# Shared expert's row tiles inside the expert loop, a shorter route, group conditions; narrow blocks' weights fetched by transfers that the scalar engine issues

## What is computed

```
def swiglu(x, w_gate, w_up, w_down):
    return (jax.nn.silu(x @ w_gate) * (x @ w_up)) @ w_down
...
def moe_ffn(h, router_w, router_bias, w_gate, w_up, w_down, ws_gate, ws_up, ws_down):
...
    affinity = jax.nn.sigmoid((h @ router_w).astype(f32))
    _, idx = lax.top_k(affinity + router_bias.astype(f32), TOP_K)
    s_sel = jnp.take_along_axis(affinity, idx, axis=-1)
    gates = s_sel / jnp.sum(s_sel, axis=-1, keepdims=True) * ROUTED_SCALE
...
    def expert_block(acc, blk):
        tok, g, e = blk
        y = swiglu(h_ext[tok], w_gate[e], w_up[e], w_down[e])
        return acc.at[tok].add(y * g[:, None]), None
...
    return acc[:n_tok] + swiglu(h, ws_gate, ws_up, ws_down)
...
        x = x + g2 * moe_ffn(h2.reshape(-1, dm), *moe_w).reshape(x.shape)
```

## Time and profile before

| what | us |
|---|---|
| runs | 2946.36, 2951.84, 2951.17 |
| median | 2951.17 |
| profiled execution, its own time | 2948.95 |
| its span | 2947.2 |
| PE busy | 2262.6 (77%) |
| DVE, ACT, POOL busy | 965.4, 602.9, 569.8 |
| HBM traffic | 628 MB read, 95 MB written |

### The profile page before, as it was taken

One profiled execution on the slowest core, in us unless ns is written; L12 is line 12 of the kernel. 1 busy time (PEld: TensorE's weight loads), 2 busy tenths in 40 slices (PEclk: granted clock), 3 DMA queues, 4 the chain that ended last, 5 costly groups with the idle time before them and its releaser, 6 DMA issues. The chain is left out here.

```text
span 2947.2 us, 41851 instructions
## 1 busy us (share of the span) xinstructions
PE 2262.6 (77%) x12118; PEld 1306.1 (44%) x12119; DVE 965.4 (33%) x2075; ACT 602.9 (20%) x1018; POOL 569.8 (19%) x470
## 2 busy tenths in 40 slices
PE   3995997669596999999999406339966999988881
PEld 2893543444343444444444206337433444444441
DVE  4742237662322111211111146861232111111113
ACT  2232224330211121212212004021021211211110
POOL 2540000000102222222222130400001222222322
PEclk9998999879797999999999757557987999999996
DMA  9983100100509999999999274314035999999994
GB/s 321 353 292 129 57 29 0 72 1 0 211 36 357 347 363 349 367 353 355 357 354 327 77 241 156 80 48 170 0 154 229 378 357 353 364 335 392 391 382 145
DMA packets 177204, 684.02 MB, mean 232 GB/s; under 512 B 34298, under 2 KB 36794, under 8 KB 132346
## 3 DMA queue, kind: packets, MB, share of 16 engines
q1 hardware_dynamic: 129642, 581.86, 51.3%
q0 software_dynamic: 38848, 71.14, 10.1%
q10 hardware_dynamic: 8624, 29.82, 2.5%
HBM read 628.15 MB, written 94.65 MB: 245 GB/s over the span
## 5 line engine op out<-in xcount | busy, mean ns | idle before, releaser
L1369 PE MATMUL pGUw_m<-wguw_m,xTw_m 128*128 128x512 f32 x800 | 358.6, 601 | 21.8 <-issue 21.8
L1380 PE MATMUL pGUn_m<-wgun_m,xTn_m 128*64 128x256 f32 x2816 | 323.3, 382 | 27.9 <-issue 27.9
L1380 PEld LDWEIGHTS pGUn_m<-wgun_m,xTn_m 128*64 128x64 f32 x2816 | 210.9, 137 | 171.7 <-issue 98.2
L1369 PEld LDWEIGHTS pGUw_m<-wguw_m,xTw_m 128*128 128x128 f32 x800 | 149.1, 191 | 232.7 <-issue 232.7
L1419 PE MATMUL pYn_m<-wdn_m,hidTn_m 128*64 128x512 f32 x704 | 189.9, 615 | 19.0 <-DVE hidTn_m L1324 16.6
L1398 PE MATMUL pYw_m<-wdw_m,hidTw_m 128*128 128x512 f32 x400 | 191.8, 602 | 15.5 <-DVE hidTw_m L1310 15.5
L1173 POOL DMA_INDIRECT xgw_m<-moe_h,idxw_m x58 | 60.4, 1042 | 652.1 <-PE pTw_m L1355 619.7
L819 POOL MEMSET zero_r<- 128x1024 f32 x2 | 1.9, 951 | 793.2 <-POOLq L69 523.7
L1179 POOL DMA_INDIRECT xgn_m<-moe_h,idxn_m x96 | 101.1, 1054 | 249.9 <-DVE idxn_m L1300 212.0
L1200 POOL DMA_INDIRECT moe_acc<-yn_m,idxn_m x88 | 140.5, 1597 | 27.5 <-issue 27.5
L1307 DVE TENSOR_TENSOR hidw_m<-hsilw_m,pGUw_m 128x256 f32<-128x256 f32 x50 | 21.1, 421 | 329.2 <-ACT hsilw_m L1242 329.2
(11 more groups left out here) (378 smaller groups left out, 3498.8 us busy)
## 6 DMA issues: line engine op xcount, KB each, us to landing
wgun_m<-in_exp_w_gate SPq DMA_DIRECT2D x88, 1024.0 KB
wgun_m<-in_exp_w_up SPq DMA_DIRECT2D x88, 1024.0 KB
wdn_m<-in_exp_w_down SPq DMA_DIRECT2D x88, 1024.0 KB
wguw_m<-in_exp_w_gate SPq DMA_DIRECT2D x50, 1024.0 KB
wguw_m<-in_exp_w_up SPq DMA_DIRECT2D x50, 1024.0 KB
wdw_m<-in_exp_w_down SPq DMA_DIRECT2D x50, 1024.0 KB
w_p<-in_mod_w SPq DMA_DIRECT2D x24, 2048.0 KB
acc_c<-moe_acc SPq DMA_DIRECT2D x30, 512.0 KB, 10.8
```

The costliest lines, as they stand in the source:

```text
L1369: last = pe.matmul(pGU_w[:], xT_w[b % 2][:, k, :], wgu[0][b % WIDE_RING][:, :, k, :], start=(k == 0), stop=(k == KD - 1))
L1380: last = pe.matmul(pGU_n[H * side:H * side + H, b % 2], xT_n[b % 2][:, k % 4, H * (k // 4):H * (k // 4) + H], w[:, :, k, P * side:P * side ...
```

## The change

- **Route.** The shared expert leaves it. PE waits for the router's two loads only (`wload` at 32), and logits of tile t-1 follow the transposes of tile t. `moe_acc` is zeroed in `mixer0`, by six transfers of SP (15.7 MB) that follow the load of the output weights; each layer has accumulators of its own. The table no longer passes DRAM: eight matmuls by the identity move it to one partition of PSUM, and DVE copies it. The copies that split the gates stand behind the table.
- **Loop.** A whole trip stands under `If(n_both > 6q)`, n_both being the larger item count. The shared expert writes `moe_shared`: its tile 0 in the prologue (row transposes first, `up` one k at a time between the picks, `down` behind them), its tile q+1 in trip q at block 3, with PE behind `rest_narrow`; ACT and DVE have it last in the block. For it the step `wide_stored`, which holds a wait at block 3 alone, stands under an `If` in every block.
- **Narrow weights.** Their ring has 2 buffers instead of 3, and ACT issues them: gate and up behind `silu_narrow`, down behind Y's evacuation, each under an `If` with a table load. The first two narrow items' six transfers are the first thing ACT does in the block.
- **Buffers.** Wide rows have 2 buffers instead of 3, `y_w` one instead of two, narrow `pGU` one; the narrow picks share a bank with it.
- **Combine.** It has four parts; PE adds three of them by the identity in PSUM (12 instructions a tile) in place of POOL; loads of tile t>=2 wait for tile t-2's sum.
- **Prepare.** The four groups' `pK` matmuls write to four column groups of the array, with the group as the innermost loop; ACT copies them in four pieces, and the stored table is 120 KB instead of 60 KB a half batch.

```diff
-WIDE_RING, NARROW_RING = 2, 3
+WIDE_RING, NARROW_RING = 2, 2
+SHARED_AT = 3
...
-            sp.wait_ge(tab_done, 1)
-            sp.dma_start(tab_dram, tabi[:]).then_inc(tab_out, 16)
-            sp.wait_ge(tab_out, 16)
-            sp.dma_start(table[:], tab_dram[0:ROWS, :].rearrange("(o a) b -> o (a b)", o=1)).then_inc(tab_in, 16)
-            for t in range(NT):
-                sp.wait_ge(y_done, t + 1)
-                sp.dma_start(accs[0][t * P:(t + 1) * P, :], ysh[:, t % 2, :]).then_inc(y_out[t % 2], 16)
...
-            act.wait_ge(zero_done, 1)
-            for acc in accs[1:]:
-                for t in range(NT):
-                    act.dma_start(acc[t * P:(t + 1) * P, :], zero[:]).then_inc(zero_out, 16)
...
+            rows(0)
+            pe.wait_ge(wload, 32)
+            for t in range(1, NT):
+                rows(t)
+                logits(t - 1)
+            logits(NT - 1)
...
+            for c in range(8):
+                last = pe.matmul(pTab[:, c, 0:ROWS], tabf[:, c:c + 1], ident[:, 0:ROWS], start=True, stop=True)
+            last.then_inc(tab_mm, 1)
...
+            n_both = eng.value_load(table[0:1, 3:4], min_val=(NT - 1) * UNROLL, max_val=max(most_wide, NE))
...
+                with eng.If(n_both > q * UNROLL):
...
+                            elif b == kind - 2:
+                                with eng.If(q < NT - 1):
+                                    step(q)
...
+                with act.If(n_narrow > i + NARROW_RING):
+                    gate_up_narrow(expert(act, 1, i + NARROW_RING), b % NARROW_RING)
...
+                act.wait_ge(yw_added, i * 16 + 32)
+                act.activation(y_w[:], pY_w[:], ACT.Copy, scale=gslot[0][b][:]).then_inc(W['y_done'], 1)
...
+                with act.If(n_narrow > i + NARROW_RING):
+                    down_narrow(expert(act, 1, i + NARROW_RING), b % NARROW_RING)
...
+            def shared_rows(t):
+                for half in range(2):
+                    act.wait_ge(Z['xT_mm'], t * 2 + 1 + half)
+                    act.activation(xT_s[:, 4 * half:4 * half + 4, :], pT_w[:].rearrange("p (k c) -> p k c", c=P),
+                                   ACT.Copy).then_inc(Z['xT_done'], 1)
...
+                act.wait_ge(Z['gu_mm'], t + 1)
+                act.activation(hsil_w[:], pGU_w[:, 0, :], ACT.Silu).then_inc(Z['silu_done'], 1)
+                act.wait_ge(Z['y_mm'], t + 1)
+                act.activation(xy_s[:], pY_w[:], ACT.Copy).then_inc(Z['y_done'], 1)
...
+            for b in range(NARROW_RING):
+                with act.If(n_narrow > b):
+                    gate_up_narrow(expert(act, 1, b), b)
+                    down_narrow(expert(act, 1, b), b)
...
+            shared_rows(0)
+            shared_rest(0)
...
+            def shared_head(q):
+                shared_rows(q + 1)
+                for k in range(KD):
+                    last = shared_up(k)
+                last.then_inc(Z['gu_mm'], 1)
...
+            def wide_stored(i, q, b):
+                if b == SHARED_AT:
+                    pe.wait_ge(W['y_done'], i + 2)
...
+            shared_rows(0)
             for i in range(AHEAD):
                 for kind in range(2):
+                    if i:
+                        pe.wait_ge(S[kind]['idx_done'], i)
                     pick(kind, i)
-                    pe.wait_ge(S[kind]['idx_done'], i + 1)
+                    last = shared_up(2 * i + kind)
+            last.then_inc(Z['gu_mm'], 1)
+            for kind in range(2):
...
+            trips(pe, n_wide, n_narrow,
+                  ((0, up_wide), (1, up_narrow), shared_at(SHARED_AT + 1, shared_stored), (0, rest_wide), (1, rest_narrow),
+                   shared_at(SHARED_AT, shared_head), (0, wide_stored), shared_at(SHARED_AT, shared_tail)))
...
+                if t >= 2:
+                    sp.wait_ge(summed, t - 1)
+                for k in range(4):
+                    sp.dma_start(slot(k, t), parts[k][t * P:(t + 1) * P, :]).then_inc(acc_in[t], 16)
...
+                pe.wait_ge(acc_in[t], 64)
+                if t >= 2:
+                    pe.wait_ge(summed, t - 1)
+                for half in range(2):
+                    c = slice(half * 512, (half + 1) * 512)
+                    for k in range(1, 4):
+                        last = pe.matmul(pS[t % 2][:, c], ident[:], slot(k, t)[:, c], start=(k == 1), stop=(k == 3))
+                last.then_inc(part_sum, 1)
...
+                dve.tensor_tensor(total[t % 2][:], slot(0, t), pS[t % 2][:], ALU.add).then_inc(summed, 1)
...
-                    for g in range(4):
-                        gg = n * GB + 4 * half + g
-                        for d, k0, c0 in ((1, 1, 0), (0, 0, 7 * SI)):
-                            for part in range(2):
-                                last = pe.matmul(pK[0:SI, g * 256 + c0:g * 256 + c0 + SL * SI], Bd[d][:, part, gg, :],
+                    for d, k0, c0 in ((1, 1, 0), (0, 0, 7 * SI)):
+                        for part in range(2):
+                            for g in range(4):
+                                last = pe.matmul(pK[32 * g:32 * g + SI, c0:c0 + SL * SI], Bd[d][:, part, n * GB + 4 * half + g, :],
```

More of the change, by code:

```diff
@@ L1002, in _, with rows @@
             pe.wait_ge(consts, 12)
-            pe.wait_ge(wload, 80)
-            for t in range(NT):
+            def rows(t):
                 pe.wait_ge(h_done, t + 1)
@@ L1057, in _ @@
-            for t in range(NT):
-                if t + 1 < NT:
-                    gate_up(t + 1)
-                down(t)
-                if t == 1:
-                    ranks()
-def moe_loop(nc, io, st, layer, n_tok, rank, pick_rhs, iota_slot, table, ident, row_base):
+            rows(0)
[4 more added lines that the diff above has]
+            logits(NT - 1)
+            pe.wait_ge(mask_done, 1)
+            pe.wait_ge(aff_done, 1)
@@ new lines, in _ @@
+            for t in range(NT + 1):
+                col = pL[:, t * NE:(t + 1) * NE]
+                for u in range(min(t + 1, NT)):
+                    last = pe.matmul(col, (upper if u == t else ones)[:], maskb[:, u, :],
+                                     start=(u == 0), stop=(u == min(t + 1, NT) - 1))
+            last.then_inc(rank_mm, 1)
+            pe.wait_ge(tab_done, 1)
+            for c in range(8):
+                last = pe.matmul(pTab[:, c, 0:ROWS], tabf[:, c:c + 1], ident[:, 0:ROWS], start=True, stop=True)
@@ L1070, in moe_loop @@
+            last.then_inc(tab_mm, 1)
+def moe_loop(nc, io, st, layer, n_tok, rank, pick_rhs, iota_slot, table, ident, row_base, wsgu, wsd):
     NT = n_tok // P
@@ new lines, in down, with shared_rows @@
+            def down(i, q, b):
+                e = expert(sp, 0, i)
+                sp.wait_ge(W['y_mm'], i + 1)
+                sp.dma_start(wd[0][b % WIDE_RING][:], w_down[bass.ds(e, 1)].rearrange("e (p k) n -> p (e k) n", k=2))\
+                  .then_inc(d_loaded[0][b % WIDE_RING], 16)
+            def shared_rows(q):
+                sp.wait_ge(Z['y_out'], q * 16 + 16)
+                first = nc.s_assert_within((q + 1) * P, P, (NT - 1) * P,
+                                           skip_runtime_bounds_check_because="the step stands under q < NT - 1")
+                sp.dma_start(xy_s[:], h_dram[bass.ds(first, P), :]).then_inc(Z['rows_in'], 16)
@@ L1166, in _ @@
+            sp.dma_start(xy_s[:], h_dram[0:P, :]).then_inc(Z['rows_in'], 16)
+            trips(sp, count(sp, 0), count(sp, 1), ((0, gate_up), (0, down), shared_at(1, shared_rows)))
         @block.gpsimd
@@ L1681, in _ @@
             t4 = v[:, 4]
+            for b in range(2):
+                dve.memset(KT[b][:], 0.0).then_inc(S['kt_zero'], 1)
             dve.wait_ge(S['par_mm'], 1)
```

373 lines of the change are left out of this document (182 added, 191 removed).

## The result

The changed kernel takes 3059.1 us (median of 4 runs, 3053.7 to 3062.1) against 2951.5 before: a ratio of 1.036 (95% interval 1.034 to 1.039), 108 us slower. I had forecast slower, 2984, with a range to 3030. The side was right, the size was not: 33 us were forecast and 108 came, so 75 are to be explained.

The account below looks back on a forecast made before the run. It took PE to bound the loop. Prepare -24, layer 0 +17.5, layer 1 +22.5 and every block +17 summed to +33, from a median of 2951.17 to 2984 us; the 8-in-10 range was 2915 to 3030.

Parts of the forecast that it names:

- What bounds the kernel: In the loop PE sets the pace, no transfer ends its waits, and work added to PE lengthens the loop in full.
- Prepare, -24: Prepare stage: pK in column groups overlaps, and the stage ends at about 205 instead of 229; bounds 0 and -34.
- zeroing in `mixer0`: Zeroing moved into mixer0, where the DMA engines are idle: 0.
- Routes, -66 and -43: Routes of layers 0 and 1: without zeroing and shared tiles they shorten by 66 and 43 us; layer 0's bounds -55 to -70.
- Tiles, +18 each and +16 a prologue: Shared tiles moved into the loops: 18 us each (bounds 15 and 20), and 16 a prologue (bounds 8 and 20).
- Trips, -33: Layer 0's loop: 30 empty blocks of 1.14 us fall away, less 1 for conditions; layer 1's skipped trips give -13.
- The If, 0.15: One more If on PE behind the narrow Y: 0.15 us in each of 88 blocks, +13; bounds 0 and 0.28 each.
- ACT's issues, +4 in the paired blocks: ACT issuing between silu and evacuation costs 0.08 us in each of 50 paired blocks, +4; bounds 0 and +25.
- Combine, +10.5 and +8.5: Combine of layers 0 and 1 with PE adding: 10.5 and 8.5 us longer; layer 0's goes from 48 to 58.5, bounds 0 and +16.
- 6.8 us a tile: Combine: each tile takes 6.8 us after a first landing at 10 us.
- The narrow ring of 2, 0: Narrow-only blocks: two buffers cost nothing, with 11.3 us of lead against a landing within 8 to 10 us.
- In every block: +17: Both loops' blocks: PE's extra If (+13) and ACT's issues in paired blocks (+4) cost 17 us together.

Follow-up runs that it names:

- e12: The kernel before the change with only prepare's pK matmuls put in column groups: 2927.3 us.
- e4: The changed kernel without the shared expert's tiles 1 and up, the combine reading tile 0's result for every tile (not the layer's result): 2858.3 us.
- e5: e1 with the narrow weights issued by SP again instead of ACT, the ring still 2: 2997.1 us.
- e7: e1 without the condition on whole trips, so that all 12 and 11 trips run: 3068.0 us.
- e3: The changed kernel without the empty If of wide_stored on PE, the step standing at block 3 alone: 3043.1 us.
- e6: e1 with the combine's loads issued all at once, four accumulator buffers for all tiles and no wait for a sum: 2993.0 us.
- e11: The changed kernel with the edits of e1, e3, e5 and e6 together: 2960.1 us, ratio 1.0025 to the kernel before.
- e1: The changed kernel with 48 never-run DVE instructions ahead of layer 1's loop: 3012.7 us.

## Why the prediction was right and wrong

- **What bounds the kernel:** right. PE set the pace in the loop, and work added to it lengthened the loop in full.
- **Prepare, -24:** right, -23.2 in the ledger and -23.7 alone (e12). PE now has gaps there, some 6 us that end on `w_p` and as much on DVE's tables; the DMA engines stand at 0.99 and DVE is busy 98 of the 106 us from 86 to 192. So DVE is a second bound beside the transfers, which I hadn't named. I priced the zeroing in `mixer0` at 0 because the DMA engines idle there: their share from 237 to 762 is 0.11 before, and 0.15 from 237 to 740 in the change.
- **Routes, -66 and -43:** right but for 5, -60.6 and -41.6. The sigmoid came 40.0 us behind the start, not 36.
- **Tiles, +18 each and +16 a prologue:** right, 17.0 to 17.4 (e4), and 16.0 and 15.6. That the prologue's total fits is in part luck. Its steps in layer 0, from the loop's start (887.7 before, 803.9 in the change) to the first `up_wide`: the first pick comes 9.7 us behind the start against 2.9, +6.8 where I had 7.6. The eight picks' starts span 16.9 us against 18.3, though `up` now stands between them, so the gaps do hide it. From the last pick to the wide rows' transposes 12.9 us pass against 1.9, +11.0 where I had 8.4, and from there to `up_wide` 6.8 against 7.3. ACT's sixth issue ends 6.3 us behind the start, as forecast, and the first evacuation of rows follows it at once, but PE itself could transpose the rows only at 807.53, released by their load; the issues cost 2.6 and 3.0 us (e5), not 7.6:

```profile
807.53 1.13 PE L1442 MATMUL pTw_m<-ident_l,xys_m 128*128 128x128 f32 x4 [7.87 <-DMA xys_m<-moe_h]
...
809.73 0.41 ACTq L1189 DMA_DIRECT2D wdn_m<-in_exp_w_down  x1
810.33 0.60 ACT L1231 ACTIVATE xTs_m<-pTw_m 128x512 f32<-128x512 f32 x1 [30.08 <-issue]
...
835.98 0.67 PE L1452 MATMUL pHI_m<-ident_l,hidw_m 128*128 128x128 f32 x2 [2.71 <-DVE hidw_m L1324]
837.17 6.35 PE L1457 MATMUL pYw_m<-wsd_l,hidTw_m 128*128 128x512 f32 x8 [0.52 <-DVE hidTw_m L1326]
```

The half clock that I took for `down` stands in both traces. First the kernel before, over all picks and the first transposes of rows, then the change, over most of `down`, whose eight matmuls take 6.35 us against the 3.70 of a tile in the loop:

```profile
888.00:915.00 27.00, 10.23 (x63) 7.91 (x64) 12.16 (x34) 1.63 (x3) 12.53 (x17) 0.50 0.89 356
```

```profile
837.00:841.50 4.50, 4.33 (x5) 1.85 (x6) 0.12 (x1) 0.00 (x0) 0.00 (x0) 0.50 0.82 330
```

- **Trips, -33:** -30.6 in layer 0. In layer 1 only 6 of 13 came: the gap there is 11.0 us against 17.0. The empty blocks that stay are dearer than the 1.14 us that I gave them (e7); how much of the missing 7 that is, no run shows.
- **The If, 0.15:** 0.22 (e3), +16 instead of +13 (a row of narrow-only blocks had said up to 0.28). ACT's issues, +4 in the paired blocks: 0 in blocks without a shared tile (e5).
- **Combine, +10.5 and +8.5:** mis-sized, +16.8 and +12.4. The step that failed is "6.8 us a tile", which measured 7.8 (47.0 us from the first matmul to the last in layer 0): I priced transfers and clock apart and let them overlap. The wait for the sum drains the queue (the DMA share is 0.29 from 1710 to 1717), 7.4 us pass from issue to the next pair's first matmul, and PE's clock falls back each time: it is 0.50 from 1704 to 1708, 1.00 from 1710 to 1717 and 0.50 again from 1721 to 1726. So both of the prediction's prices, half clock behind idle time and full clock later, occur in every pair. e6 gets back 19.7. The sum was also told incompletely: 10 + 6 x 6.8 is 50.8 and not 58.5. The 7.7 us between are the work behind PE's last matmul, which the text doesn't name; measured, 7.6.
- **The narrow ring of 2, 0:** right in the changed kernel, where no wait of the narrow up ends on a transfer, with little to spare: the up weights landed 11.0 us behind their issue (median of all 88; 10.0 from 2640 to 2990), where I had 8 to 10 and a lead of 11.3. In e4 it cost some 6 us and in e11 about one. The forecast also has a 0 for the narrow weights coming from ACT's queue instead of SP's, which no row of the kernel before shows; measured, layer 0's 28 periods without a shared tile take 584.5 us with ACT's issues and 585.0 with SP's, and the gap in narrow-only blocks is 0.95 with both (e1, e5).
- **The step that failed outright** is one that the prediction doesn't have. "In every block: +17" counted what each added instruction costs where it is executed. It has no term for DVE, and took instructions as free that are passed by. The loop on DVE became six instructions longer, and none of the added ones runs in the narrow-only trips; at the place where it stands DVE then fetched code anew in each of six trips (29 packets of the instruction queue, each trip's with DVE's stalls; none in e1). That is 46.2 of the 58 us by which layer 1's narrow-only periods exceed the forecast (350.0 here, 303.8 in e1): 33 are PE's longer gaps, 13 the longer matmuls behind them at the lower clock. Of the other 12, the If's higher price is 3 (7.7 measured, 5 forecast), and some 5 are the longer gaps ahead of block 4 and at each trip's start, which e3 keeps; about 4 are not explained.
- With it went the range: it was built from the bounds of priced steps, and no bound covered a cost of another kind. That the forecast had the right side owes nothing to this cost: without it e1 stands at 3012.7, 29 above the forecast and inside the range.

## What to carry to other kernels

Moving work from a stretch where the bounding engine is partly idle into one where it is full gained nothing by itself here; price the work in both places, with the gaps it has there (11.6 us against 17.4 here), before looking at what the move frees. When a change adds code to a long device-side loop, compare the instruction transfers inside the loop before and after: a stall ended by "issue" once per trip, at the same block, was the mark, and moving that engine's code was the cure here. In the routes here, where TensorE worked in pieces of 2 us at a granted clock of 0.50 and 96 small matmuls followed at the same clock (20.6 us, against 10.8 at 1.00), filling the gaps gave 24 us and starting later 11: in such a stage both are worth trying.

## What was not expected of the hardware

- DVE's time depended on instructions that it never runs: 48 of them ahead of a loop of 309 took 46 us away (3059.1 to 3012.7), while a loop of 303 at the same start had no such stall (2952.7).
- DVE began 2.4 to 4.2 us behind its input at each of the twelve stalls, in a stretch where the DMA engines were busy for 0.86 to 0.89 of the time, and the fetches come in packets of 8 KB (29 packets, 0.24 MB).
- TensorE ran its 96 logit matmuls in 20.6 us behind pieces of 2 us with gaps of 0.6, and in 10.8 us behind 9 us of work with gaps of no more than 0.22. The granted clock of the slow ones was 0.50 to their end, although they ran without a gap. Starting the engine 10 us later made the kernel 11 us faster.
